# GpSimd's low part of the second query half queued behind VectorE's low parts, and all four token tiles turned ahead of the key products

## The reference, cut to what matters

```python
h = rmsnorm(x, norm1_g)                  # x: 512 x 1024
proj = h @ w_in                          # w_in: 1024 x 4352
q, k, v, cb, cc, cx, g_attn, g_conv = jnp.split(proj, SPLIT_POINTS, axis=-1)
q = rmsnorm(q.reshape(b, s, N_HEADS, HEAD_DIM), q_norm_g)      # 512 columns
k = rmsnorm(k.reshape(b, s, N_KV_HEADS, HEAD_DIM), k_norm_g)   # 128 columns, v as many
...                                      # windowed attention, gated convolution, merge,
                                         # then a mixture of 32 experts, then the second block
```

## Time and profile before

| | before |
|---|---|
| median of 3 runs | 1994.71 us (1994.18 to 1997.05) |
| profiled execution, its own time | 1996.16 us |
| its span, first to last instruction | 1994.4 us |
| TensorE busy | 1874.3 us, 94% |
| VectorE busy | 1025.2 us, 51% |
| ScalarE busy | 815.9 us, 41% |
| GpSimd busy | 565.5 us, 28% |
| mean granted clock of TensorE | 0.981 of full speed |
| read from HBM | 241.89 MB |

### The profile page before, as it was taken

How to read it: one execution, slowest core, us unless ns; L and a number is a source line. 1 busy time by engine, 2 the same in 40 slices (tenths; PEclk the granted TensorE clock), 3 DMA queues, 4 the chain that set the end, 5 groups by cost and what they waited for, 6 DMA issues and landing times.

```text
span 1994.4 us, 28241 instructions
## 1 busy us (share of the span) xinstructions
PE 1874.3 (94%) x11002; PEld 1467.3 (74%) x11002; DVE 1025.2 (51%) x2029; ACT 815.9 (41%) x1551; POOL 565.5 (28%) x401
## 2 busy tenths in 40 slices
PE   6999999998778999988999999999899999999998
PEld 5878889832223893457988888899767798888886
DVE  4170443521113625873376676822567625676777
ACT  4122651311012413364554544353366636544443
POOL 4244431011110420144421123233045643113211
PEclk8999999999889999999999999999889999999999
DMA  6222403799999330201123223321203012223321
GB/s 236 86 85 86 168 1 149 267 401 419 421 420 353 128 107 0 85 1 44 43 100 112 85 85 127 123 71 44 43 2 86 2 43 85 85 85 127 126 85 43
DMA packets 86869, 252.10 MB, mean 126 GB/s; under 512 B 12212, under 2 KB 19700, under 8 KB 74448
## 3 DMA queue, kind: packets, MB, share of 16 engines
q1 hardware_dynamic: 81344, 238.79, 32.5%
q0 software_dynamic: 4592, 9.30, 1.3%
q10 hardware_dynamic: 800, 2.20, 0.3%
HBM read 241.89 MB, written 15.73 MB: 129 GB/s over the span
## 4 chain that ended last, share of the span: by engine, by line
PE 48%; DVE 3%; ACT 3%; issue 2%; POOL 0%; DVEq 0%; ACTq 0%
PE psA L1517 32%; PE psO L2170 2%; PE psO L1686 2%; PE psT L1686 2%; PE psS L1686 2%; PE psT L2211 2%; ACT big L2239 1%; DVE x L2835 1%; PE psA L1635 1%; PE psS L2200 1%; PE psA L2200 1%; PE psO L1583 1%; PE psT L1615 1%; ACT tok L2239 1%; PE psA L2080 1%
## 5 line engine op out<-in xcount | busy, mean ns | idle before, releaser
L1215 POOL TENSOR_TENSOR w_slot<-ring,w_slot 128x1024 fp32r<-128x1024 f32 (+2 forms) x80 | 208.7, 2624 | 539.9 <-ACT w_slot L2239 539.6
L1517 PE MATMUL psA<-hT_hi,w_slot 128*128 128x512 f32 x960 | 297.8, 389 | 0.0
L2239 ACT ACTIVATE w_slot<-ring 128x1024 fp32r<-128x1024 f32 (+2 forms) x178 | 191.9, 1088 | 178.4 <-PE psA L1517 78.4
L1517 PEld LDWEIGHTS psA<-hT_hi,w_slot 128*128 128x128 f32 x960 | 180.2, 188 | 37.2
L2835 DVE TENSOR_TENSOR x<-psA,x 128x512 f32<-128x512 f32 (+1 forms) x206 | 122.4, 623 | 140.1 <-PE psA L1517 135.5
L1517 PE MATMUL psA<-hT_lo,w_slot 128*128 128x512 f32 x480 | 186.7, 389 | 0.0
L2835 DVE TENSOR_TENSOR w_slot<-ring,w_slot 128x1024 fp32r<-128x1024 f32 x98 | 119.9, 1225 | 115.6 <-ACT w_slot L2239 115.6
L2239 ACT ACTIVATE big<-psA 128x512 f32<-128x512 f32 (+7 forms) x145 | 63.9, 465 | 246.1 <-PE psA L1517 141.1
L1517 PE MATMUL psA<-w_slot,hid_part 128*128 128x512 f32 x672 | 161.4, 389 | 0.0
L2239 ACT ACTIVATE scr<-scr,stat 128x384 f32<-128x384 f32 (+3 forms) x224 | 124.4, 556 | 74.1 <-DVE stat L3798 44.4
L1517 PEld LDWEIGHTS psA<-w_slot,hid_part 128*128 128x128 f32 x672 | 126.1, 188 | 26.2
(11 more groups left out here) (465 smaller groups left out, 4491.5 us busy)
## 6 DMA issues: line engine op xcount, KB each, us to landing
ring<-in_mlp_w SPq DMA_DIRECT2D x32, 2048.0 KB, 8.3
ring<-in_w_in SPq DMA_DIRECT2D x8, 2048.0 KB, 8.2
ring<-in_w_gate_e SPq DMA_DIRECT2D x14, 1024.0 KB, 15.7
ring<-in_w_up_e SPq DMA_DIRECT2D x14, 1024.0 KB, 20.8
ring<-in_w_down_e SPq DMA_DIRECT2D x13, 1024.0 KB, 28.3
big<-in_w_down_e SPq DMA_DIRECT2D x12, 1024.0 KB
ring<-in_ab_w_in SPq DMA_DIRECT2D x5, 2048.0 KB, 9.2
scr<-in_w_down_e SPq DMA_DIRECT2D x7, 1024.0 KB
```

The costliest lines, as they stand in the source:

```text
L1215: nc.gpsimd.tensor_tensor(part(w_lo, c), raw_piece(c), part(w_hi, c).bitcast(F32), ALU.subtract)\
L1517: ins = pe.matmul(o, a, b, start=(at == 1), stop=(at == 3 * len(terms)))
L2239: return nc.scalar.activation(o, i, f, **kw)
```

## The change

Two things. GpSimd waits, ahead of its second piece (`c == 1`), until VectorE has counted `early_in_lo` to KD = 8. And the order at the start is another one: the key product of tile 0 gets its number behind all turned tiles, as the other three, so that TensorE turns all four tiles first and no longer waits for the eviction of "vec"; ScalarE evicts "vec" after the last tile's root, rounds the first query half before any key eviction, and evicts tile 0's key product after three chunks and tile 1's after all eight; VectorE takes the four means first and then the eight multiplications, without the wait for tile 0's key product that stood ahead of the last. Nothing is computed in another way.

```diff
--- before.py
+++ after.py
@@ -137,7 +137,7 @@
 JOBS, WIDTH = {}, {}
 _at = 0
 for _n, _w in (("vec", 1),
-               ("norm0", KD + 1), ("kv", NT - 1), ("q", 2 * NT), ("cc", 4), ("cx", 4), ("cb", 4), ("ga", KD),
+               ("norm0", KD), ("kv", NT), ("q", 2 * NT), ("cc", 4), ("cx", 4), ("cb", 4), ("ga", KD),
                ("gc0", 4), ("gc1", 4), ("mergec", KD), ("mergea", KD), ("wo", 3 * NT), ("tail1", NT + KD),
                ("ranks", 1), ("table", 1), ("gates", 1), ("moe", 5 * PAIRS), ("late", 2),
                ("norm2", KD), ("ai", 2 * NT), ("aq", 2 * NT), ("bv", 2 * NT), ("turn_small", 4), ("kh", 4), ("vh", NT),
@@ -170,8 +170,6 @@
     if stage == "nq":
         name, first = ("nqa", 0) if i < NT else ("nqb", NT) if i < 3 * NT else ("nqc", 3 * NT)
         return JOBS[name] + i - first
-    if stage == "kv":
-        return JOBS["kv"] + i - 1 if i else JOBS["norm0"] + 3 * 2
     if stage == "nk":
         return JOBS["nk"] + i - 1 if i else JOBS["tail4"] + NT + 3 * 2
     n = i - WIDTH[stage]
@@ -182,7 +180,7 @@
 
     if n in TAIL.values():
         return JOBS[f"tail{n}"] + (3, 6, 8, 11 if n == 4 else 10)[t] + half
-    return JOBS[f"norm{n}"] + 2 * t + half + (n == 0 and t == NT - 1)
+    return JOBS[f"norm{n}"] + 2 * t + half
 
 
 APART = {norm_turn(n, t, half): (t, half) for n in (0,) + SPLIT_NORMS for t in range(NT) for half in range(2)}
@@ -307,7 +305,7 @@
         plan.append((name, [(0, SLOT, SLOT // src.shape[1], 0, SLOT // src.shape[1], src)], last))
 
     w_in = w["w_in"][0]
-    for name, c0, c1, last in (("kv", 512, 768, ("kv", NT - 1)), ("q", 0, 512, "q+7"), ("cc", 1280, 1792, "cc+3"),
+    for name, c0, c1, last in (("kv", 512, 768, "kv+3"), ("q", 0, 512, "q+7"), ("cc", 1280, 1792, "cc+3"),
                                ("cx", 1792, 2304, "cx+3"), ("cb", 768, 1280, "cb+3"),
                                ("ga0", 2304, 2816, "ga+3"), ("ga1", 2816, 3328, "ga+7"),
                                ("gc0", 3328, 3840, "gc0+3"), ("gc1", 3840, 4352, "gc1+3")):
@@ -1227,6 +1225,8 @@
                 pool.wait_ge(rstd_ready, t + 1)
                 nc.gpsimd.tensor_scalar(tok[:, t, :], x[:, t, :], rstd[:, t:t + 1], one, ALU.mult, ALU.mult).then_inc(normed, 1)
             for c in range(SPLIT_AT["cp"]):
+                if c == 1:
+                    pool.wait_ge(early_in_lo, KD)
                 split_weight(c)
 
             for m in range(4):
@@ -1691,20 +1691,16 @@
 
             pe.wait_ge(const_loaded, CONST_LOADS * 16)
             turn(JOBS["vec"], [vec_rows[:, :]])
-            copied(pe, JOBS["vec"])
-            for t in range(NT - 1):
-                norm_tile(0, t)
+            norm(0)
             need("kv")
             for t in range(NT):
-                o = begin(job("kv", t))
+                o = begin(JOBS["kv"] + t)
                 for half in range(2):
                     copied(pe, norm_turn(0, t, half))
                 for k in range(KD):
                     ins = pe.matmul(o[:, 0:256], hT[:, k, t * P:(t + 1) * P], slot("kv")[:, k * 256:(k + 1) * 256],
                                     start=(k == 0), stop=(k == KD - 1))
                 ins.then_inc(proj_ready, 1)
-                if t == 0:
-                    norm_tile(0, NT - 1)
             pe.wait_ge(early_in_hi, KD)
             pe.wait_ge(early_in_lo, KD)
             split_token_major("q", "q", 0, chunks(hT_lo_early), high=chunks(hT_hi_early))
@@ -2442,7 +2438,7 @@
 
             def kv_out(t):
 
-                n = job("kv", t)
+                n = JOBS["kv"] + t
                 product(act, n)
                 A(qk[:, t, 512:640], bank(n)[:, 0:P], ACT.Copy)
                 A(v1[:, t, :, 0:HD], bank(n)[:, P:2 * P].rearrange("p (g d) -> p g d", g=2), ACT.Copy)\
@@ -2455,20 +2451,17 @@
             for t in range(NT):
                 first_squares(t)
                 first_root(t)
-                if t == 1:
-                    evac(JOBS["vec"], vec[:, :], 64)
+            evac(JOBS["vec"], vec[:, :], 64)
             copied(act, JOBS["vec"])
             act.wait_ge(const_loaded, CONST_LOADS * 16)
-            for half in range(2):
-                copied(act, norm_turn(0, NT - 2, half))
-            kv_out(0)
             split_weight(SPLIT_AT["q"])
             for half in range(2):
                 copied(act, norm_turn(0, NT - 1, half))
             for k in range(KD):
-                if k == 6:
-                    kv_out(1)
+                if k == 3:
+                    kv_out(0)
                 A(hT_hi_early[:, k, :], hT[:, k, :], ACT.Copy).then_inc(early_in_hi, 1)
+            kv_out(1)
             split_weight(SPLIT_AT["q"] + 1)
             kv_out(2)
             kv_out(3)
@@ -2894,8 +2887,8 @@
                 g = GAINS[NORMS[n]]
                 for half in halves:
                     m = norm_turn(n, t, half)
-                    if n in (0, TAIL["mlp0"]) and (t, half) == (NT - 1, 1):
-                        copied(dve, job("nk" if n else "kv", 0))
+                    if n == TAIL["mlp0"] and (t, half) == (NT - 1, 1):
+                        copied(dve, job("nk", 0))
                     if n in SPLIT_NORMS and 2 * t + half >= 6:
                         dve.wait_ge(normed_lo_first, 2 * SPLIT_NORMS.index(n) + 2 * t + half - 5)
                     dst = turned_whole(t, half) if n in SPLIT_NORMS else hT[:, 4 * half:4 * half + 4, t * P:(t + 1) * P]
@@ -3172,13 +3165,11 @@
             nc.vector.memset(u[:, :, 0:T + 2:T + 1], 0.0)
             nc.vector.memset(v1[:, :, :, HD:HD + 1], 1.0)
 
-            for t in range(NT - 1):
+            for t in range(NT):
                 norm_scale(0, t)
             dve.wait_ge(const_loaded, CONST_LOADS * 16)
             copied(dve, JOBS["vec"])
-            norm_whole(0, 0)
-            norm_scale(0, NT - 1)
-            for t in range(1, NT):
+            for t in range(NT):
                 norm_whole(0, t)
             for half in range(2):
                 copied(dve, norm_turn(0, NT - 1, half))
@@ -3193,7 +3184,7 @@
                                           evac_to(n)[:, 0:256].rearrange("p (j d) -> p j d", j=4))\
                         .then_inc(proj_evacuated[n % 2], 1)
             copied_all(dve, "q", 2 * NT)
-            copied_all(dve, "kv", WIDTH["kv"])
+            copied_all(dve, "kv", NT)
             qk4 = qk.rearrange("p t (h d) -> p (t h) d", d=HD)
             squares = a1["ga"][:, 0:NT * 640].rearrange("p (t n) -> p t n", t=NT)
             sq4 = squares.rearrange("p t (h d) -> p t h d", d=HD)
```

## The result

The changed kernel takes 1984.99 us (median of 7 runs, 1979.36 to 1986.33), the kernel before 1994.71 us (median of 7, 1991.25 to 1998.27). One execution of experiment 5 was slow (3574.96 us) and stands in none of the ratios. The profiled spans are 1983.2 and 1994.4 us. The prediction was 1983.6 us, in a range from 1981.0 to 1987.0.

A forecast was written before the change was run, and what follows sets the result against it. TensorE, busy 94% of the span, was taken as the bound, idle while VectorE's low parts waited for GpSimd. Idle time of 9.5 us plus 1.6 us of clock gave 1994.71 - 11.1 = 1983.6 us, range 1981.0 to 1987.0.

The forecast's parts named there:

- The reading of the collisions: Early low parts: VectorE's and GpSimd's subtractions of two SBUF tensors exclude each other, each waiting for the other's whole instruction.
- The start of the query products: TensorE's first query product comes at 29.8 us, 30.7 at most, instead of 39.26.
- The clock: Behind TensorE's idle gap the lower clock disappears, worth 1.6 us up to the first query copy.
- The sum: Start of the kernel: 9.5 us of TensorE idle time and 1.6 us of lower clock, together 11.1 us.
- The landing of the query weight: The query weight lands at 17.1 us, so ScalarE rounds it until 19.0; landing at 19.24 gives a start near 30.7.
- The rounding of the query weight: Late-weight rival: rounding ends after 20.4 and VectorE's chain ends last; two us late give 1985.6 us; chance 0.08.
- The case of "more": Rival: earlier uninterrupted work raises TensorE's clock before 15 us, 1.4 us more gain, 1982.2 us; chance 0.10.
- swallowed: Rival: the DMA-bound stage of 370 to 650 us ends when it did, 1994.7 us; chance 0.04.
- slower: Rival: DMA engines move less from 370 to 650 us; at 375 GB/s the time is 1999.3 us; chance 0.03.
- The point against: GpSimd's subtractions now run beside VectorE's query copies; cost taken as zero, other bound 0.4 us.
- The value of the parts: Start of the kernel: the wait alone gives 10.1 us, the new order alone 2 to 4 us.
- That the shift reaches the end: The whole shift reaches 220 us and passes the DMA-bound stage of 370 to 650 us, so the same 11 us remain.

The follow-up runs named there:

- experiment 5: The changed kernel with GpSimd's wait ahead of its second piece at four of VectorE's low parts instead of eight; ratio 0.9997 to the kernel before.
- Experiments 1: The kernel before with GpSimd's wait alone, order of turned tiles and evictions unchanged; 1984.98 us, ratio 0.9948 to the kernel before.
- experiment 4: The kernel before with GpSimd's two query pieces each in four subtractions instead of one; 1990.45 us, ratio 0.9977 to the kernel before.
- experiments 2: The changed kernel without GpSimd's wait, so the new order alone; ratio 1.0002 to the kernel before.
- experiment 7: The changed kernel with 17 added products of zeros on TensorE ahead of its first turning; ratio 0.9946 to the kernel before.
- experiment 3: The kernel before with 38 added identity products in TensorE's idle gap ahead of the first query product; ratio 1.0002 to the kernel before.
- experiment 6: The changed kernel with the wait ahead of GpSimd's first piece instead of its second; 1980.65 us, ratio 0.9933 to the kernel before.

## Why the prediction was right, point by point

**The reading of the collisions was right.** The low parts were forecast as one near 4.6 us and seven of 0.68, ending near 28.4; they were 4.53 and seven of 0.68, ending at 28.63. GpSimd's second piece was to follow within 0.2 us and take 4.55 us; it followed after 0.08 us and took 4.63. Experiments 1 and 4 show the cause by itself, from two sides, and experiments 2 and 5 that neither the order alone nor a start behind four parts does it.

**The start of the query products** was put at 29.8 and was 29.02. Three small terms make up the difference: the first input came 0.22 us earlier than in the run before; tile 3 was turned in 1.12 instead of 1.3 us; and I took the recorded end of the last key product (30.03) as the moment at which the next can begin, but the next one begins about 0.35 us ahead of that end, as the rows show (15.39 + 13.98 = 29.37, and 29.02). That last one is the term that was mis-sized by a wrong reading of a row.

The forecast read the lower clock for the first tiles from their time alone and said that no granted clock was on record there. The column does have a value there, 1.00, as in experiment 7; the reading is borne out by that experiment and not by the column.

**The clock** was put at 1.6 us. Here it is the time from the first product to the first copy, 4.68 us before and 3.21 now: 1.47, and 1.6 by experiment 3.

**The sum** was 11.1 us; at the first copy it is 11.7, at the end of the profiled span 11.2, by the times 10.8 (8.0 to 13.6).

**The range** had luck in it. It allowed 1.2 to 1.4 us of scatter, after three executions within 2.9 us. There are two kinds of executions, some 5 to 6 us apart (last section), and these three were all of the long kind. So were six of the seven of the changed kernel; the seventh, 1979.36 us, lies below the range, and so does the median of experiment 6 (1980.65 us), which has the same mechanism and more executions of the short kind.

**The landing of the query weight** carried the choice between 29.8 and 30.7. ScalarE's row

```profile
17.32 1.91 ACT L2235 ACTIVATE q_w_hi<-ring 128x2048 fp32r<-128x2048 f32 x1 [6.58 <-DMA ring<-in_w_in]
```

puts it at 17.3, against 17.1 from the landing's row.

**The rivals.** The rounding of the query weight ended at 19.2, short of the 20.4 from which the chain of low parts would have set the start. The case of "more" was made in experiment 7: it gave 0.2 us and not 1.4, because TensorE's own work already ended near 29 and the low parts at 28.7. Nothing was swallowed or slower in the expert stage.

**The point against** was answered with zero, without a row: the query copies now run beside GpSimd's subtractions, at 32.23 and 35.06 under pieces from 28.71 to 38.04, and take 0.42 us as before. So these VectorE copies out of PSUM were not held back by GpSimd's subtractions in SBUF.

**The value of the parts** was right for the wait (10.1 us forecast, 10.4 measured) and wrong for the order alone (2 to 4 us forecast, no gain in the times and 0.7 us at the first copy). Two terms failed there, though three parts were stopped as forecast. One is the start of the query products, put at 35 to 37 and measured at 37.77: the stopped parts and the free ones together took as long as before, 17.35 us. The other is the price of the restart: I took 1.6 us of lower clock from the trace of before, and the restart cost 2.3 us in experiments 2 and 5 (5.48 and 5.49 us to the first copy, against 3.2 without a gap). What decides between 1.5 and 2.3 us stays open.

**That the shift reaches the end** was right: the fixed points of SP's queue keep it through the expert stage to 0.15 us.

## What to carry to other kernels

Where VectorE and GpSimd both subtract SBUF tensors, look in the trace for VectorE instructions whose end follows a GpSimd instruction's end by their own short duration: each such one waited for the whole of it. Put the long GpSimd instruction behind the short ones that the critical engine waits for, if it has slack (here 7 us: it ended at 33.3, and TensorE asks for it with its fifth tile, at about 40.3), and if it has none, cut it into shorter instructions, which here gave back 4.6 of 10 us. And an idle gap on TensorE costs its length and the lower clock behind it, between 1.4 and 2.3 us here.

## What the runs showed of the hardware that was not expected

- **The clock can fall after the work is back.** In experiment 4 the gap was 4.9 us and TensorE restarted at 34.09 at its upper level, 2.4 GHz. Half a us later the clock was at 1.2 GHz, with TensorE fully busy:

```profile
34.10:34.60 0.50, 0.50 (x4) 0.50 (x5) 0.00 (x0) 0.50 (x1) 0.50 (x1) 0.97 0.11 24
34.60:38.00 3.40, 3.40 (x18) 3.40 (x17) 0.00 (x0) 3.40 (x8) 3.40 (x2) 0.50 0.48 158
```

  The first copy came 4.62 us after the first product, as after the gap of 9.2 us (4.68).

- **Turning alone got faster, as by a rise of the clock.** In the changed kernel TensorE does nothing but turn tiles from 9.09 to 15.39, and the fourth takes 1.12 us (14.27 to 15.39) where the three before take 1.73 each; in experiment 5, whose turning began at 8.64, the fourth takes 0.88. That this is the clock is read from these times and experiment 7, since the clock's column reads 1.00 throughout. The Trainium skill, "TensorE: Matmul & The Clock Gate", section "Part 4: PE-mode transpose", says that the upper level of the clock doesn't engage for transposes, since they don't count as TensorE being busy in the same way (its transposes were bf16, these are float32); here the fourth tile was sped up with nothing ahead of it but the turned vector rows and tiles. The measurement decides.

- **A phase of the clock far from the change moves the time by 3 us and more.** The executions of the changed kernel are six between 1983.2 and 1986.3 us, at a mean granted clock of 0.983 or 0.984, and one of 1979.36 at 0.987. The profiled execution of experiment 7 was one of the short kind (span 1977.5). Between 1370 and 1500 us its clock is higher than that of the changed kernel (first row), for nearly the same work:

```profile
1370.00:1500.00 130.00, 118.27 (x996) 99.56 (x995) 75.93 (x270) 64.95 (x185) 40.43 (x62) 0.92 0.08 17
```
```profile
1370.00:1500.00 130.00, 117.94 (x1034) 99.41 (x1033) 80.07 (x282) 68.82 (x195) 43.46 (x66) 0.96 0.11 22
```

  From the load of the last output weights of the second block to the store of the result it took 577.3 us (1390.22 to 1967.55), the changed kernel 580.7 us (1392.58 to 1973.26). Experiment 7 is another kernel, though its first copy is only 0.3 us earlier, and no trace of a short execution of the changed kernel was taken. The kernels before and changed and those of most experiments have executions of both kinds, 3 to 6 us apart; what decides between them stays open. It is why the intervals are as wide as they are. Within a kind the effects come out more sharply. Beside the changed kernel, the kernel before has five executions from 1994.2 to 1998.3 us and two near 1991.3; the medians of the long kind and those of the short kind are both 12 us apart. Beside experiment 4, the kernel before has medians of 1996.5 and 1990.7 (long, short), the quarters 1991.5 and 1985.3: 5.0 and 5.4 us. The division was made after the times were known, and by them.
